# Mixing stage of an RWKV-7 and attention step: the head sums of the squared keys as two rounded products

## What is computed

```python
rkvg = jnp.einsum('pbtd,pde->pbte', xs[:4], w_in)
r, k, v, g = rkvg[0], rkvg[1], rkvg[2], rkvg[3]
wl = (w0 + jnp.tanh(xs[4] @ w1) @ w2).astype(f32)
decay = jnp.exp(-jnp.exp(-jax.nn.softplus(-wl) - 0.5))
a = jax.nn.sigmoid((a0 + (xs[5] @ a1) @ a2).astype(f32))
kk = heads(k.astype(f32) * k_k.astype(f32))
kk = kk / jnp.maximum(jnp.sqrt(jnp.sum(kk * kk, -1, keepdims=True)), 1e-12)
kf = k.astype(f32) * (1.0 + (a - 1.0) * k_a.astype(f32))
```

## Time and profile before

| | |
|---|---|
| median of 3 runs | 1488.85 us (1484.57 to 1491.69) |
| profiled execution | 1487.88 us |
| its span | 1486.1 us, 37540 instructions |
| mean granted PE clock | 0.982 |
| PE busy | 1421.5 us (96%) |
| DVE busy | 799.2 us (54%) |
| ACT busy | 578.8 us (39%) |
| POOL busy | 242.1 us (16%) |

### The profile page before, as it was taken

How to read it: one execution, slowest core, us unless ns; L and a number is a source line. 1 busy time by engine, 2 the same in 40 slices (tenths; PEclk the granted TensorE clock), 3 DMA queues, 4 the chain that set the end, 5 groups by cost and what they waited for, 6 DMA issues and landing times. The chain is left out here.

```text
span 1486.1 us, 37540 instructions
## 1 busy us (share of the span) xinstructions
PE 1421.5 (96%) x16154; PEld 1291.7 (87%) x16154; DVE 799.2 (54%) x1591; ACT 578.8 (39%) x1181; POOL 242.1 (16%) x343
## 2 busy tenths in 40 slices
PE   6999999999999899999999989999999999998997
PEld 6989898888899799999999958889999998665785
DVE  6737245777821377776777464561111122776545
ACT  6726246887821122222122332441111132886324
POOL 0000000000000355664556320000000100214000
PEclk9999999999999999999999789999999998999999
DMA  5724122567692245543553146024334236521202
GB/s 205 223 59 103 59 88 89 160 174 225 193 265 81 59 110 117 116 103 82 116 117 89 52 155 222 29 88 136 87 88 112 80 105 169 163 89 48 87 29 92
DMA packets 244294, 173.47 MB, mean 117 GB/s; under 512 B 148735, under 2 KB 218303, under 8 KB 243215
## 3 DMA queue, kind: packets, MB, share of 16 engines
q1 hardware_dynamic: 212167, 156.12, 36.6%
q10 hardware_dynamic: 31968, 15.04, 3.5%
HBM read 110.97 MB, written 60.46 MB: 115 GB/s over the span
## 5 line engine op out<-in xcount | busy, mean ns | idle before, releaser
L361 PE MATMUL mix_acc<-mix_high,mix_w_high 128*128 128x364 f32 (+1 forms) x768 | 177.4, 339 | 13.3 <-DVE mix_w_low L592 13.3
L361 PE MATMUL mix_acc<-mix_low,mix_w_high 128*128 128x364 f32 (+1 forms) x768 | 171.4, 331 | 0.6 <-DVE mix_low L578 0.6
L361 PE MATMUL mix_acc<-mix_high,mix_w_low 128*128 128x364 f32 (+1 forms) x768 | 170.3, 330 | 0.0
L361 PEld LDWEIGHTS mix_acc<-mix_high,mix_w_high 128*128 128x128 f32 x768 | 129.7, 189 | 31.9 <-issue 17.7
L361 PEld LDWEIGHTS mix_acc<-mix_low,mix_w_high 128*128 128x128 f32 x768 | 132.5, 189 | 1.3 <-DVE mix_low L578 0.9
L361 PEld LDWEIGHTS mix_acc<-mix_high,mix_w_low 128*128 128x128 f32 x768 | 133.1, 188 | 0.0
L1473 PE MATMUL out_acc<-qkvg_room_r_high,qkvg_room_w_high 128*128 128x364 f32 (+1 forms) x320 | 106.4, 333 | 3.0 <-issue 1.9
L592 DVE TENSOR_TENSOR mix_w_low<-mix_wt,mix_w_high 128x1024 fp32r<-128x1024 f32 x32 | 39.2, 1224 | 125.3 <-ACT mix_w_high L433 125.0
L1473 PE MATMUL out_acc<-qkvg_room_r_low,qkvg_room_w_high 128*128 128x364 f32 (+1 forms) x320 | 105.8, 331 | 0.0
L1473 PE MATMUL out_acc<-qkvg_room_r_high,qkvg_room_w_low 128*128 128x364 f32 (+1 forms) x320 | 105.8, 330 | 0.0
L447 ACT ACTIVATE mix_out<-mix_acc 128x364 f32<-128x364 f32 (+1 forms) x96 | 38.3, 472 | 152.6 <-PE mix_acc L361 152.5
(11 more groups left out here) (276 smaller groups left out, 3431.5 us busy)
## 6 DMA issues: line engine op xcount, KB each, us to landing
mix_wt<-in_w_in SPq DMA_DIRECT2D x32, 512.0 KB, 4.4
qkvg_room_wt<-in_w_att SPq DMA_DIRECT2D x20, 512.0 KB, 4.1
delta_bk<-scr_bk SPq DMA_DIRECT2D x17, 512.0 KB, 4.7
delta_kr<-scr_kr SPq DMA_DIRECT2D x17, 512.0 KB, 7.2
scr_kr<-mix_outs SPq DMA_DIRECT2D x16, 512.0 KB, 3.6
scr_bk<-mix_outs SPq DMA_DIRECT2D x16, 512.0 KB, 4.5
early_xpad<-in_xpad SPq DMA_DIRECT2D x8, 548.5 KB, 8.6
scr_xg<-early_xs SPq DMA_DIRECT2D x8, 544.0 KB, 3.0
```

What stands on the lines that cost most here:

```text
L361: mm = pe.matmul(acc[:, s, k, 0:width], w[:, s, d, :], r[:, d, n0:n0 + width], start=d == 0 and q == 0, stop=d == DT - 1 and q == 2)
```

## The change

The squares are split into `square_high` (rounded, written by ACT from the key once more) and `square_low` (`square` less `square_high`, by DVE). `sum_heads` makes two rounded matmuls for each column part, with a rounded copy of the 0/1 matrix, `ones_of_heads`, which ACT makes once. `square_low` lies on the place of `square`, `square_high` on that of `norm`; so the second square waits until the last key's norms have been used (L651). The sum moves one step back, behind step 4, in the key jobs; in job 24 it stays behind step 4.

```diff
+        with Tensors(nc, "parts") as parts:
+
+            parts.sb("before", 128, 14 * N)
+            square_low, square_high = (parts.sb(x, 128, N, dtype=F32R) for x in ("square_low", "square_high"))
...
+        ones_of_heads = m.sb("ones_of_heads", 128, 128, dtype=F32R)
...
-        LORA2_AT, SUM_AT = {0: 0, 2: 1, 3: 2, 4: 3}, 3
+        LORA2_AT, SUM_AT = {0: 0, 2: 1, 3: 2, 4: 3}, 4
...
                 def sum_heads(j):
                     s = j % 2
-                    pe.wait_ge(squared, j + 1)
+                    pe.wait_ge(ones_rounded, 1)
+                    pe.wait_ge(squared, 2 * j + 2)
+                    pe.wait_ge(squares_split, j + 1)
                     for k, (n0, n) in enumerate(PARTS):
-                        pe.matmul(acc[:, s, k, 0:n], headsum[:], square[:, n0:n0 + n], start=True, stop=True).then_inc(summed, 1)
+                        pe.matmul(acc[:, s, k, 0:n], ones_of_heads[:], square_high[:, n0:n0 + n], start=True, stop=False)
+                        pe.matmul(acc[:, s, k, 0:n], ones_of_heads[:], square_low[:, n0:n0 + n], start=False, stop=True).then_inc(summed, 1)
...
-                        if 1 <= j <= DT and d == (SUM_AT if j < DT else SUM_AT + 1):
+                        if 1 <= j <= DT and d == SUM_AT:
                             sum_heads(j - 1)
...
+                        if j == 0:
+                            act.activation(ones_of_heads[:], headsum[:], ACT.Copy).then_inc(ones_rounded, 1)
...
                     act.activation(square[:], out[:, j % 2], ACT.Square, scale=k_k[:, j:j + 1]).then_inc(squared, 1)
+                    if j:
+                        act.wait_ge(vec, VEC * (j - 1) + 5)
+                    act.activation(square_high[:], out[:, j % 2], ACT.Square, scale=k_k[:, j:j + 1]).then_inc(squared, 1)
...
+                def split_squares(j):
+                    dve.wait_ge(squared, 2 * j + 2)
+                    dve.tensor_tensor(square_low[:], square[:], square_high[:].bitcast(F32), ALU.subtract).then_inc(squares_split, 1)
+
...
                         if j:
                             key_step(j - 1)
+                            split_squares(j - 1)
                         if j < DT:
                             scan(j)
```

More of the change, by code:

```diff
@@ L126, in mixed_projections @@
         v_turned, v_kept, hid_acc, hid_made = (m.sem(x) for x in ("v_turned", "v_kept", "hid_acc", "hid_made"))
+        squares_split, ones_rounded = m.sem("squares_split"), m.sem("ones_rounded")
         mix_stored, staged_loaded = m.sem("mix_stored"), [m.sem(f"staged_loaded{d}") for d in range(DT)]
```

## The result

The changed kernel takes 1503.3 us, the median of 6 runs (1499.2 to 1509.6), the kernel before 1490.3 in as many (1484.6 to 1498.5). The ratio is 1.0098, with a 95% interval from 1.0074 to 1.0121: slower by 1%. The profiled execution took 1502.0 us, its span is 1500.2, 14.1 longer than before.

A forecast was written before the change was run, and what follows sets the result against it. TensorE, busy for 96% of the span, was taken as the bound, by its stream's order and few waits. Terms -0.6 + 14.9 - 0.7 - 0.9 + 1.4 = +14.1 us on 1487.9 gave 1502.0 us, range 1494 to 1508.

The forecast's parts named there:

- point 1: Sums of keys 0 to 6 on PE: rounded matmuls gain 0.82 us a key, 5.7 us in all.
- point 2: Second square ahead of ScalarE's second sigmoid: the third lora piece waits 0.4 us in six key jobs, costing 2.5 us.
- point 3: VectorE's subtraction in the key jobs delays early stores and the lora2 loads behind them: cost 2.6 us, bounds 0 and 5.
- point 4: Last key's sum in job 24: PE waits 14.9 us for the subtraction behind VectorE's other work, bounds 12.5 and 17.
- the two pushes: Job 24, delaying the last subtraction: second square ahead of `high` on ScalarE, +1.1 us; later load into `decay`, +1.2 us.
- point 5: Beside job 24's wait: shorter last sum -0.7 us, no wait of job 25's dots -0.9, slow PE clock +1.4.
- point 6: Behind the last sum: job 26's weights are split at 431.1, PE arrives at 432.4; 1.3 us of cover, no cost.
- the wait alone: Rival: loads and queues catch up and the clock costs little; +8.3 us, 1496 us, chance 0.18.
- a second wait: Rival: the thin cover breaks and PE waits 2 to 4 us more before job 26; 1506 us, chance 0.09.
- no pause: Rival: job 24's last subtraction isn't late, done by 396.3; it ends at 1486 us, no change, chance 0.04.
- The clock gives it back: Rival: the slow clock at 840 to 860 us stays at 2.4 GHz, some 8 us return; 1494 us, chance 0.09.

The follow-up runs named there:

- experiment 8: On top of experiment 7, the last key's dot products in job 25 stand behind steps 4 and 5 instead of 2 and 3: ratio 0.9946, 1480.8 us.
- its control: The kernel before with the lora2 load first and the last dots behind steps 4 and 5 of job 25, without rounded sums: ratio 0.9962, 1482.1 us.
- Experiment 4: The lora2 load issued on SyncE ahead of the early stores: ratio 1.0085 in the changed kernel, 0.9997 in the kernel before.
- experiment 7: On top of experiment 6, the second square stands behind the second sigmoid in the key jobs: ratio 0.999.
- Experiments 1: The kernel before with one added wait: key 7's sum in job 24 waits for key 7's bonus product; ratio 1.0106.
- experiment 2: The changed kernel with key 7's subtraction moved first in job 24 on VectorE, ahead of the rests of gate tiles 6 and 7: ratio 1.0033.
- experiment 6: The changed kernel with the lora2 load first, key 7's squares ahead of gate tile 5, its subtraction ahead of the rests of tiles 5 to 7: ratio 0.9988.

## Why the prediction was right, point by point

- **The product (point 1)**: 0.82 us a key was forecast. A step with the rounded sum takes 3.34 us in place of the 3.36 of the working. A key job without late loads takes 18.6 us in experiment 8 against 19.4 in its control. Right. By the four passes that the Trainium skill ("FP8 and Floating Point Precision", section TensorE Precision Notes) gives a true fp32 product, the gain would have been an estimated 1.0; the trace stays nearer to 0.8.
- **The second sigmoid (point 2)**: a wait of 0.4 us in six jobs was expected; the change has 0.9 us in three waits, for both pieces together. The costs of points 2 and 3 were not independent. Where PE waits for `lora2`, ScalarE has done its evacuation meanwhile, and the sigmoid comes earlier after the first piece. Experiment 4, which takes the loads away, brings all six waits back, and with them a key job takes 19.0 us, 0.4 more than the 18.6 of experiment 7, as forecast.
- **The loads (point 3)**: two jobs with 2.8 us more were expected (the cost was put down as 2.6); it is six jobs and 5.5 us more. I had given the others 1 to 2 us to spare, and the shift of 1.3 us and PE's own gain ate it. This room is the step of the walk that was wrong. Since the late loads hid the waits of point 2, the two points together cost less than forecast all the same: they were put at 5.1 us, and PE starts job 24 2.1 us earlier than before (385.6 for 387.7), so of the 5.7 gained 3.6 went. The keys give 2.1 us, not 0.6.
- **The last key (point 4)**: 14.9 us of wait against 15.2, with the place, the engine and the row named. The subtraction ends at 409.2, not 411.1. VectorE's wait for gate tile 6 grew by 2.2 us (3.11 for 0.87), close to the 2.3 of the two pushes, but it came to that wait 1.8 us earlier (394.6 for 396.4). I had worked out that row without the gain of the keys, which PE had as well. The wait is the difference of the two, in which this mostly drops out. Experiments 1 and 2 show that the wait is the cause.
- **Beside it (point 5)**: the shorter sum was put at -0.7 and the clock at +1.4, together +0.7. From the start of the last sum to job 25 it is 7.15 us in place of 6.43, +0.7. The same stretch takes 5.58 us in experiment 6, which has no slow clock there, so the clock costs 1.6; filling the pause gave back 1.5. The wait of the dots is gone, and job 25 is 1.0 us shorter, for 0.9 forecast. The Trainium skill, "TensorE: Matmul & The Clock Gate", section "Part 1: The HAM clock gate", says that activity releases a throttled default; the pause of the change agrees, with 0.52 behind it and 1.00 from 413 us on. The stretch of experiment 6, at 0.52 with PE busy for 8.00 of 8.00 us, does not.
- **Behind the sum (point 6)**: no second wait. The weights of job 26 are split at 429.2 and PE starts on them at 430.5, with the 1.3 us of cover that the working had. The wait came only in experiment 8, where PE was early enough.
- **The sum**: -2.1 for the keys, +15.2 for the wait, +0.7 for the last sum and the clock, -1.0 for the dots make the 12.8 us that the mixing is longer; it was put at +14.1, and the difference lies in the keys. The span is +14.1 all the same, because the rest of the program took 1.3 us more in this profile. That this fits is chance.

Of the rivals, *the wait alone*, +8.3 us, was too small, *a second wait* and *no pause* did not occur. *The clock gives it back*: the stretch of the earlier trace rows kept a slow part, some 14 us later:

```profile
854.00:862.00 8.00, 6.38 (x164) 6.27 (x162) 0.00 (x0) 0.60 (x1) 0.00 (x0) 0.66 0.36 130
862.00:870.00 8.00, 6.00 (x112) 5.48 (x110) 2.97 (x5) 2.51 (x5) 4.86 (x5) 0.70 0.01 2
```

It was shorter, about 10 us in place of 20, yet nothing came back: the rest of the program took 998.4 us, and 997.1 before. Nor do other profiles show it: with about 10 us of slow clock there in the first version of experiment 8 the rest took 997.9 us, with about 20 in its control 994.1.

## What to carry to other kernels

When a step gets a new input from another engine, look at every instance of it, the last above all: seven of eight sums found their subtraction ready, and the eighth, in a job where VectorE's queue held other work ahead, cost more than all the gain. Read from the order what stands in front of the new instruction, and compare its end with the time at which the consumer arrives. And a product that is made faster shows up only when the next waits, here a small load behind large stores and a late dot product, are moved as well.

## What the runs showed of the hardware that was not expected

The granted clock can fall after short waits, and stay down under full work. In experiment 6 a wait of 1.9 us, with small two-column matmuls behind it, was followed by some 10 us at 1.2 GHz in which PE was busy for 8.00 of 8.00 us; in experiment 7 the same wait was followed by about 6 us. A wait of 1.0 us at the same place before left it at 2.4 GHz, and so did PE's waits of 0.9 and 1.1 us for weights in experiment 8.

Nor does the price of a pause go by its length. From the start of the last rounded sum to job 25 it is 5.6 us without a slow clock (experiment 6). It is 7.1 behind the pause of 15.2 us in the change, 7.9 behind 4.7 us in experiment 2, and 8.0 behind 15.4 us in experiment 4. So in these runs a pause of this kind cost 1.6 to 2.4 us through the slow clock, and the short wait of experiment 6 cost about 5. What sets this was not tried apart from the moves above.
